# Five RMS norms of a two-chunk token tile: the square of the second chunk moves from VectorE to ScalarE

## What is computed

```
def rmsnorm(x, g):
    xf = x.astype(jnp.float32)
    y = xf * lax.rsqrt(jnp.mean(xf * xf, axis=-1, keepdims=True) + EPS)
    return y.astype(x.dtype) * g
def modulate(h, shift, scale):
    return h * (1 + scale[:, None, :]) + shift[:, None, :]
...
x = x + g1[:, None, :] * mix
h = modulate(rmsnorm(x, ffn_norm_g[layer]), sh2, sc2)
x = x + g2[:, None, :] * grouped_moe(h, router_w, router_bias, exp_w_gate[layer], exp_w_up[layer], exp_w_down[layer])
```

## Time and profile before

| | |
|---|---|
| median of 3 runs | 2266.33 us |
| the profiled execution, its own time | 2266.9 us |
| span of that execution, first to last instruction | 2265.1 us |
| PE busy | 1866.3 us (82%) |
| DVE busy | 1513.6 us (67%) |
| ACT busy | 839.3 us (37%) |
| POOL busy | 555.8 us (25%) |
| mean granted TensorE clock | 0.919 |

### The profile page before, as it was taken

The page is one execution under the profiler, slowest core; times in us unless marked ns, Lnnn a source line. Parts: engine busy times, 40 slices in busy tenths (PEclk is TensorE's granted clock), DMA queues, the critical chain, the costliest instruction groups (busy, mean ns, idle before and its releaser), DMA issues.

```text
span 2265.1 us, 22026 instructions
## 1 busy us (share of the span) xinstructions
PE 1866.3 (82%) x7603; PEld 1236.0 (55%) x7603; DVE 1513.6 (67%) x2494; ACT 839.3 (37%) x1285; POOL 555.8 (25%) x614
## 2 busy tenths in 40 slices
PE   3988699999968887999999497788677777777787
PEld 1866578888745566788887344458332232232233
DVE  3345777899863556578998898346966666676642
ACT  1353344687723532457886001233221121121110
POOL 0000100000000000203000000001777777777771
PEclk8998699999989886999999698888799989999999
DMA  9761389999945514958997233232999999999995
GB/s 321 271 223 38 132 284 305 370 374 377 342 169 211 186 38 163 190 186 318 378 364 294 108 130 111 75 130 85 396 410 409 409 409 410 409 410 409 409 409 238
DMA packets 194014, 617.19 MB, mean 272 GB/s; under 512 B 19096, under 2 KB 21568, under 8 KB 193264
## 3 DMA queue, kind: packets, MB, share of 16 engines
q1 hardware_dynamic: 114336, 325.98, 39.9%
q0 software_dynamic: 78864, 286.95, 32.9%
q10 hardware_dynamic: 704, 2.86, 0.4%
HBM read 609.43 MB, written 6.29 MB: 272 GB/s over the span
## 4 chain that ended last, share of the span: by engine, by line
PE 50%; DMA 15%; DVE 14%; issue 10%; POOL 9%; ACT 2%; DVEq 0%; SPq 0%; POOLq 0%; ACTq 0%
PE PS L955 17%; DMA peer_rows<-in_peer_u,MOD 9%; PE PS L976 8%; PE PS L760 6%; POOL peer_rows L692 4%; PE PS L781 4%; PE PS L751 4%; PE PS L1153 3%; POOL peer_rows L706 2%; POOL AR L706 2%; DMA AR<-in_peer_v,MOD 2%; DMA peer_rows<-in_peer_v,MOD 2%; DVE peer_rows L2151 1%; DMA ring<-in_w_mod 1%; DVE AR L1461 1%
## 5 line engine op out<-in xcount | busy, mean ns | idle before, releaser
L2151 DVE SCALAR_TENSOR_TENSOR peer_rows<-peer_rows,PS 128x1024 f32<-128x1024 f32 x256 | 312.3, 1220 | 213.4 <-DMA peer_rows<-in_peer_u,MOD 213.3
L1838 DVE TENSOR_TENSOR weights_low<-ring,weights_high 128x1024 fp32r<-128x1024 f32 x231 | 280.1, 1229 | 63.7 <-ACT weights_high L1270 61.2
L1270 ACT ACTIVATE weights_high<-ring 128x1024 fp32r<-128x1024 f32 x231 | 242.6, 1061 | 114.8 <-PE PS L955 78.3
L692 POOL DMA_INDIRECT peer_rows<-in_peer_u,MOD x256 | 245.3, 958 | 118.8 <-issue 63.4
L1153 PE MATMUL PS<-peer_rows,HT 128*128 128x512 f32 x376 | 186.1, 635 | 68.0 <-ACT HT L1449 40.4
L1838 DVE TENSOR_TENSOR weights_low_more<-ring,weights_high_more 128x1024 fp32r<-128x1024 f32 x153 | 185.4, 1224 | 36.3 <-ACT weights_high_more L1270 34.7
L1633 DVE TENSOR_TENSOR weights_low<-ring,weights_high 128x1024 fp32r<-128x1024 f32 (+1 forms) x81 | 95.3, 1196 | 143.4 <-ACT weights_high L1177 142.9
L1270 ACT ACTIVATE weights_high_more<-ring 128x1024 fp32r<-128x1024 f32 x153 | 161.0, 1060 | 70.8 <-PE PS L955 44.4
L1153 PEld LDWEIGHTS PS<-peer_rows,HT 128*128 128x128 f32 x376 | 71.0, 201 | 181.3 <-issue 155.5
L1443 ACT ACTIVATE MOD<-MOD 128x16 f32<-128x16 f32 x16 | 3.4, 216 | 428.6 <-DVE peer_rows L2151 428.6
L955 PE MATMUL PS<-weights_high,slots_high 128*128 128x512 f32 x386 | 156.5, 405 | 3.2 <-DVE weights_low L1838 3.2
(11 more groups left out here) (368 smaller groups left out, 3820.5 us busy)
## 6 DMA issues: line engine op xcount, KB each, us to landing
ring<-in_exp_w_gate SPq DMA_DIRECT2D x128, 512.0 KB, 5.8
ring<-in_exp_w_up SPq DMA_DIRECT2D x128, 512.0 KB, 6.0
ring<-in_exp_w_down SPq DMA_DIRECT2D x128, 512.0 KB, 5.6
ring<-in_w_mod SPq DMA_DIRECT2D x20, 2048.0 KB, 9.0
ring<-in_w_in SPq DMA_DIRECT2D x7, 2048.0 KB, 8.8
ring<-in_a_w_in SPq DMA_DIRECT2D x6, 2048.0 KB, 12.2
ring<-in_kv_w_mod SPq DMA_DIRECT2D x16, 512.0 KB, 5.7
ring<-in_w_mod SPq DMA_DIRECT2D x16, 512.0 KB, 5.4
```

Source lines behind the costliest of these rows:

```text
L692: pool.indirect_dma_start(out=u_row(k), out_offset=None, in_=A["peer_u_2"][0], in_offset=bass.IndirectOffsetOnAxis(ap=EXPERT[:, c, PT_ * h ...
L1270: A_(high_of(n0 + n), raw(ring_slot(layer, m)), ACT.Copy).then_inc(S("moe_high"), 1)
L1838: V.tensor_tensor(low_of(n0 + n), raw(ring_slot(layer, ring_no[layer, "E", n])), high_of(n0 + n).bitcast(fp32), ALU.subtract).then_inc(S(" ...
L2151: V.scalar_tensor_tensor(u_row(k), u_row(k), 1.0, PS[:, 2 * c:2 * c + 2, :].rearrange("p a k -> p (a k)"), ALU.mult, ALU.mult, accum_out=D ...
```

## The change

At the five places ScalarE squares chunk 1 with the sum in `st[:, 1:2]`, as soon as `x_ready` is there, and VectorE squares chunk 0 only; VectorE then waits for the new semaphore `square` before the small instructions. The other norms (`a`, `latent`, `q`, `n1`, and the output's) keep both squares on VectorE. To make room for the semaphore, several others are merged, with their waits' counts changed to match (`c_silu`, `c_act` into `c_ready`; `c_tp`, `cum_mm` into `early_mm`; `krope`, `ropeC` into `key_rope`; `f_exp`, `f_ln` into `f_log`; `dt`, `ssm_sin` into `ssm_act`; `ssm_ang`, `powers` into `ssm_dve`; `peerk_in` into `ssm_in`); no instruction moves for that. The diff without those:

```
+    square_no = {n: i + 1 for i, n in enumerate(["a_o", "moe0", "b_o", "moe1", "c_o"])}
...
+        def square(ready):
+
+            act.wait_ge(S("x_ready"), x_no[ready])
+            A_(H[:, 1, :], X[:, 1, :], ACT.Square, accum_out=st[:, 1:2]).then_inc(S("square"), 1)
...
         highs("a_o", STAGES)
-        mod_copies("mod0_d")
+        mod_copies("mod0_d", slice(0, 1))
+        square("a_o")
+        mod_copies("mod0_d", slice(1, 2))
         act.wait_ge(S("ang"), 1)
...
+        square("moe0")
         tp("h_kv")
...
-        mod_copies("mod1_e")
+        mod_copies("mod1_e", slice(0, 1))
+        square("b_o")
+        mod_copies("mod1_e", slice(1, 2))
         tp("h_ffn1")
         experts(1)
+        square("moe1")
 
         tp("ssm_w")
...
         highs("peer_q", 0, STAGES)
+        square("c_o")
         tp("peer_k")
...
-        def rms_scale(src, width, junk):
-
-            V.scalar_tensor_tensor(junk[:, 0, 0:width], src[:, 0, :], 1.0, src[:, 0, :], ALU.mult, ALU.mult,
-                                   accum_out=st[:, 0:1])
-            L(V.scalar_tensor_tensor(junk[:, 1, 0:width], src[:, 1, :], 1.0, src[:, 1, :], ALU.mult, ALU.mult,
-                                     accum_out=st[:, 1:2]))
+        def rms_scale(src, width, junk, squared=None):
+
+            for c in range(1 if squared else C):
+                last = V.scalar_tensor_tensor(junk[:, c, 0:width], src[:, c, :], 1.0, src[:, c, :], ALU.mult, ALU.mult,
+                                              accum_out=st[:, c:c + 1])
+            L(last)
+            if squared:
+                wait("square", square_no[squared])
             ts(st[:, 2:4], st[:, 0:2], 1.0 / width, ALU.mult, EPS, ALU.add)
             inverse_root(st[:, 4:6], st[:, 2:4], st[:, 6:8])
...
-        rms(X, D, H, "ffn0", shift=mod_part(3), signal="h_ready")
+        rms(X, D, H, "ffn0", shift=mod_part(3), signal="h_ready", squared="a_o")
```

More of the change, by code:

```diff
@@ L676, in _ @@
         for half, k_ in enumerate(("peer_k1_2", "peer_k2_2")):
-            pool.dma_start(KN[:, half::2, :], A[k_][0].rearrange("h n d -> n h d")).then_inc(S("peerk_in"), 16)
+            pool.dma_start(KN[:, half::2, :], A[k_][0].rearrange("h n d -> n h d")).then_inc(S("ssm_in"), 16)
         load_gain("nf")
@@ L999, in _ @@
         pe.wait_ge(S("consts_in"), 16)
-        pe.wait_ge(S("c_silu"), 1)
-        nc.tensor.transpose(PS[:, 7, 0:DB], cN[:, :], ident[0:DB, 0:DB]).then_inc(S("c_tp"), 1)
-        pe.wait_ge(S("c_act"), 1)
+        pe.wait_ge(S("c_ready"), 1)
+        nc.tensor.transpose(PS[:, 7, 0:DB], cN[:, :], ident[0:DB, 0:DB]).then_inc(S("early_mm"), 1)
+        pe.wait_ge(S("c_ready"), 2)
         gemm_mod("mod0_a")
@@ L1021, in _ @@
                                         start=False, stop=True)
-        last.then_inc(S("cum_mm"), 1)
+        last.then_inc(S("early_mm"), 1)
         mod_total(*beside[5])
@@ L1047, in _ @@
         gemm("kv_up", CKVT, ht("ckv"))
-        tp("kB", ("krope", 1), evac_at[stages["kv_up"][-1][0]])
+        tp("kB", ("key_rope", 1), evac_at[stages["kv_up"][-1][0]])
         tp("cq", per_chunk=("cq", 1))
@@ L1127, in _ @@
         gemm("c_o", None)
-        tp("peer_k", ("peerk_in", 32))
+        tp("peer_k", ("ssm_in", 16 * (2 * 2 + 8 * 2 + 6 + 1) + 32))
         tp("h_n2", per_chunk=("h_ready", h_no["n2"]))
@@ L1317, in _ @@
         act.wait_ge(S("c_in"), 16)
-        A_(cN[:, :], cN[:, :], ACT.Silu).then_inc(S("c_silu"), 1)
-        act.wait_ge(S("c_tp"), 1)
-        A_(cT[:, :], PS[:, 7, 0:DB], ACT.Copy).then_inc(S("c_act"), 1)
+        A_(cN[:, :], cN[:, :], ACT.Silu).then_inc(S("c_ready"), 1)
+        act.wait_ge(S("early_mm"), 1)
+        A_(cT[:, :], PS[:, 7, 0:DB], ACT.Copy).then_inc(S("c_ready"), 1)
         mod_copies("mod0_a")
@@ L1336, in v_out @@
                 act.wait_ge(S("f_abs"), 1)
[L1337 to L1339 removed]
+                A_(Ft, Ft, ACT.Exp, scale=-1.0).then_inc(S("f_log"), 1)
+                act.wait_ge(S("f_log"), 1)
+                A_(Ft, Ft, ACT.Ln, bias=ones[:, 0:1]).then_inc(S("f_log"), 1)
             return to_rows(z["V"])(i - 1, banks)
         evac("a_v", v_out, beside=lambda i: i and mod_copies("mod0_b", slice(3 + i, 4 + i)))
[L1342 removed]
+        act.wait_ge(S("early_mm"), 2)
         cum = PS[:, 7, 0:C * HEADS].rearrange("p (c h) -> p c h", c=C)
@@ L1651, in ssm_parameters @@
             lr, li, dt, x, t, ang, ex, sn, sh, xc, p_, m_, em, cm, r_, ar_, ai_, dd, fr, fi, er, u_ = SP_[:22]
-            wait("dt", 1)
+            wait("ssm_act", 1)
             tt(x, lr, dt, ALU.mult)
@@ L1669, in ssm_parameters @@
             yield
-            wait("ssm_sin", 1)
+            wait("ssm_act", 2)
             ts(ex, ex, BIG, ALU.min, -1.0, ALU.add)
@@ L1921, in _ @@
         lows("a_v", STAGES + 4)
-        wait("f_ln", 1)
+        wait("f_log", 2)
         V.tensor_tensor(F, F, Ft, ALU.subtract).then_inc(S("logf"), 1)
@@ L1938, in _ @@
         scale_gain("kv", KM[:, D:2 * D])
-        rms(X, D, H, "kv", shift=KM[:, 0:D], signal="h_ready")
+        rms(X, D, H, "kv", shift=KM[:, 0:D], signal="h_ready", squared="moe0")
         wait("mod_out", MOD_GROUPS)
@@ L1956, in _ @@
                 L(last)
-        last.then_inc(S("krope"), 1)
+        last.then_inc(S("key_rope"), 1)
         rms(CKV[:, :, 0:KVR], KVR, CKV[:, :, 0:KVR], "latent", junk=HTm[:, 0:512].rearrange("p (c d) -> p c d", c=C),
@@ L1981, in _ @@
         add_product("b_o", mod_part(2))
-        rms(X, D, H, "ffn1", shift=mod_part(3), signal="h_ready")
+        rms(X, D, H, "ffn1", shift=mod_part(3), signal="h_ready", squared="b_o")
         add_mod1("mod1_e")
@@ L1985, in _ @@
         gated_add(Y, mod_part(5), "moe1")
-        rms(X, D, X, "final", junk=H)
+        rms(X, D, X, "final", junk=H, squared="moe1")
         rms(X, D, H, "n1", signal="h_ready", gain=MOD[:, 0:D])
@@ L2049, in _ @@
                 L(last)
-        last.then_inc(S("ropeC"), 1)
+        last.then_inc(S("key_rope"), 1)
         skip(3)
@@ L2086, in _ @@
         add_product("c_o", None)
-        rms(X, D, H, "n2", signal="h_ready")
+        rms(X, D, H, "n2", signal="h_ready", squared="c_o")
         lows("peer_q", 0, STAGES)
```

18 lines of the change are left out of this document (9 added, 9 removed).

## The result

| | before | after |
|---|---|---|
| median | 2266.45 us (6 runs, 2263.49 to 2267.42) | 2254.84 us (6 runs, 2253.08 to 2259.02) |
| the profiled execution, its own time | 2266.9 us | 2253.08 us |
| its span | 2265.1 us | 2251.3 us |
| mean granted TensorE clock | 0.919 | 0.922 |
| DVE busy | 1513.6 us | 1507.5 us |

The medians are 11.6 us apart. The ratio of the runs is 0.9955 [0.9944, 0.9967], an interval of 7.5 to 12.7 us. The sign was right and the size was half. The profiled execution after is the fastest of its six, so its trace shows a larger difference (13.8 us) than the medians.

A forecast was written before the change was run, and what follows sets the result against it. The prediction took five VectorE squares on the chain, with ScalarE free beside them, as the bound: 5.80 less 0.15 us of waits, 5.65 us, takes the profiled 2266.9 to 2261.25, by medians 2260.7 us; range 2258.0 to 2264.2.

The forecast's parts named there:

- the path: At five norms, VectorE's square of chunk 1 stands on the chain, 1.16 us each, 5.80 us in all.
- The sum of the prediction: Over the five norms: 5.80 us off VectorE less 0.15 us of added waits, 5.65 us won.
- ScalarE's price: Square of chunk 1 with its read on ScalarE: 1.15 us lower bound, 1.23 upper; the lower was taken.
- The added wait: VectorE's wait for `square` before the small instructions: 0 to 0.06 us a place, 0.03 taken, 0.15 in all.
- The rival with chance 0.10: Square needs its own table set on ScalarE, 1.28 us per load; only 2.5 us won, 2263.8 us; chance 0.10.
- The rival with chance 0.12: The two squares slow each other, 0.3 us or more at four places, or gains vanish further down; chance 0.12.
- the covers: ScalarE's copies delayed behind the squares hold nothing up: some 3.2 us spare at a_o, 3 at moe1, 1.8 at c_o.
- the merged semaphores: Merging semaphores moves no instruction and costs nothing; the replaced waits were for the same events in the same order.
- The clock, slower: Later starts shift against TensorE's granted clock; over 0.2% slower from 20 us more low clock; chance 0.04.
- under 1 us each: Gain at a_o and b_o if a chunk's eight transposes (1.49 us) run at 2.4 GHz after shorter idle time.
- the prediction's own formula: Low-clock time of the whole kernel from its mean clock: 0.081 x 2 x 2265 = 367 us at 0.50.
- the three runs lie within 0.95 us: The small spread of the kernel before's runs, given as evidence against a slowdown by the clock.

The follow-up runs named there:

- e3: Changed kernel with VectorE squaring chunk 0 twice at the five places, so its path is as long as before; 2267.34 us, ratio 1.0005 to the kernel before.
- e1: Kernel before with only the merged semaphores, no square moved to ScalarE; 2265.84 us, ratio 1.0004 to the kernel before.
- e10: Kernel before with dummy TensorE products in idle time (seven before the slots' products, six at n1, ten around n2's transposes); 2258.84 us, ratio 0.9962.
- e12: Kernel before with fewer dummy TensorE products (five before the slots' products, one before the gates', four at n1); 2253.50 us, ratio 0.9942.
- e13: Changed kernel with the same shortened set of dummy TensorE products as e12; 2249.94 us, ratio 0.9924 to the kernel before.
- e4: Kernel before with the square moved to ScalarE at a_o alone; 2264.34 us, ratio 0.9992 to the kernel before.
- e7: Kernel before with the square moved to ScalarE at moe1 alone; 2264.87 us, ratio 0.9989 to the kernel before.
- e11: Changed kernel with the same longer set of dummy TensorE products as e10; 2254.86 us, ratio 0.9944 to the kernel before.
- e2: Changed kernel run and profiled again without any edit; 2255.24 us, ratio 0.9952 to the kernel before.
- e9: Changed kernel with three small VectorE copies after the wait for the square at each of the five places; 2259.20 us, ratio 0.9960 to the kernel before.

## Why the prediction was half right

**Right: the path.** The sum of the prediction, five times 1.16 less the waits, describes what happened up to the end of each norm: VectorE's small instructions come 1.15 us sooner after X at each of the five places (2.45 to 1.30 at a_o, b_o and moe1, 4.15 to 3.00 at moe0, 2.56 to 1.41 at c_o), 5.7 us in all. e3 shows that the result rests on it.

**Right: ScalarE's price.** Lower bound 1.15 us, taken; measured 1.06 us and a read that begins 0.09 us before its end, and the two squares ended together. The added wait was put at 0.03 us a place; 1.15 us won instead of 1.16 leave 0.01 for it.

**Right: no table load, no disturbance.** The rival with chance 0.10 is out: five squares, at places where Copy, Exp and Silu had run, and no load before one. The Trainium skill, "ScalarE: Activation LUTs", section "Table sets: the hidden batching unit", doesn't name square among the functions that are in every set. These runs show that no switch is needed at these five places. The rival with chance 0.12 is out too: VectorE's square takes 1.23 us with ScalarE's beside it.

**Right: the covers.** At a_o, moe1 and c_o the delayed copies held up nothing on the path; the stage after c_o, the thinnest cover, was 1.4 us shorter.

**Right: the merged semaphores** (e1).

**Wrong: the paragraph "The clock, slower", and with it a term missing from the sum.** It had the mechanism (a shift of every later start against whatever moves the clock) and the price (half of each microsecond at the low clock), and then treated it as something that averages out: a chance of 0.04 for slower and 0.04 for better by over 8 us in all, "under 1 us each" for the only gain that was worked out. The runs showed a term of 11.6 - 5.65 = 6.0 us by the medians, as large as the sum itself (1.8 to 7.0 us by the interval of the ratio). e10 and e12 show that this clock can be moved alone and what it is worth: 7.7 and 13.4 us with the squares untouched. The mean clock agrees: 0.917 in the median of the 74 executions of the kernel before that ran beside the experiments, 0.922 in that of the changed kernel's eleven. By the prediction's own formula (1 - 0.922) x 2 x 2251.3 = 351 us in place of 367, or of 376 at 0.917: 16 to 25 us less, worth up to 8 to 12 where TensorE's work bounds.

Three readings led there. First, "the three runs lie within 0.95 us" was taken as evidence that the clock does little. A small spread speaks against luck and not against an effect: in some stages the clock repeats itself from execution to execution. The stage after a_o took 415.06 to 415.65 us in the seven kernels whose norm ended as late as before, so its low stretches are a property of the program and change with the program. And the small spread was itself luck: with three more runs it was 3.9 us, and over the 74 executions beside the experiments 8.1 us (2261.64 to 2269.76), at mean clocks of 0.913 to 0.922. Second, the window 235 to 245 in the earlier trace rows was read as "the clock is low after the norm" and not followed to its end. The low stretch ends at 265.8, 6.5 us into the slots' products. At that edge work is priced double, and the change moves work across it. Third, the rows that would have shown the way, rows of 1.48 and of 0.85 us for four products of the same kind, were there before the change.

**What stays open.** Why the clock rises where it does is not shown: only that at a_o it fell after TensorE had idled, was low through the router's products (7 us of busy time), and rose 6.5 us into the slots' products before, 4.4 us into them after the change, and during the dummies in e10 to e13. Why the low stretch began sooner in e4 is open; its stage ahead of a_o was 2.3 us longer than in the kernel before, but so it was, or more, in e7 (5.3) and e10 (2.5), where the stretch began 8.0 to 8.1 us after X. Why the stage after moe0 differed in e11 and e12 is open too. The stage after moe1 took from 258.7 to 261.3 us in unchanged code, so that e7's gain there (-1.8 us by medians) can't be split. c_o has its own single run only, and its stage is not made shorter by less low clock (e10). The 3.6 us between e12 and e13 are explained up to the first expert's product and not behind it.

## What to carry to other kernels

When a change moves the moment at which dense TensorE work begins after an idle time, price the work at the edge: find in the windows where the granted clock rises again, see which products lie before that edge, and ask how many the change moves over it. Cut the program at instants that repeat (here the five sums into X) and compare stage lengths: where a stage shrinks by more than the work taken from its path, compare its low stretches before and after. And where TensorE waits for another engine ahead of dense work, a few dummy products in the wait, short enough to end before the real ones are due, can be worth as much as a shorter wait: 13.4 us of 2267 here, beside 11.6 for five norms.

## What the runs showed of the hardware that was not expected

- The granted clock can be repeatable in a stage and vary over the program. The stages after a_o and b_o have the same low stretches (30.7 and 6.8 us; 27.3 and 3.4 after the change) in separate executions and separate kernels, and that after b_o took 419.33 to 419.45 us in seven kernels. The stage ahead of a_o, with the same work, took 227.1 to 232.4 us in fifteen executions, and the kernel before took 2261.64 to 2269.76 us.
- At a_o the low stretches came in few lengths: 20.5, 27.3 and 30.7 us for the first, 3.4 and 6.8 for the second. A norm that ended 1.15 us sooner took 3.4 us off each in the changed kernel and in e2, and nothing in e4; one that ended 0.56 us later (e9 against the changed kernel) changed neither.
- The router's 32 products, 6.98 us in e10, ran within the low stretch, and the clock was still low behind them.
- Less low clock is not always less time: after c_o, 51.2 us in e10 against 71.7 before, and the same stage length within 0.12 us.
- A Square of 128x1024 with its sum takes ScalarE 1.057 us and 0.185 for the read, no table load, and does not slow VectorE's square of the other half of the same tile (1.23 us with and without it).
